# Leaving the last attention step of each tile without a piece of the top-k search, in a one-core hybrid decoder layer

## The chip, the core and the metric

The kernel runs on one core of a Trainium2 chip. The metric is device time in microseconds for one execution of the whole layer; the time of a kernel is the median of several executions, and the profile is a further single execution. TensorE (PE) does the matmuls and the transposes. VectorE (DVE), ScalarE (ACT) and GpSimd (POOL) do the elementwise work, and SyncE (SP) issues the DMAs. Each engine works through its own instructions in the order in which they are written and waits on semaphores for the others.

## What is computed

One decoder layer over 2048 positions of width 1024: a mixing sub-layer (sparse attention beside a pooling mixer), a squared-ReLU MLP, and a gated per-layer embedding. The change touches the sparse attention alone. A cheap indexer scores all keys of a query, the 256 best causal keys are kept, and eight heads attend to those:

```python
logits = jnp.einsum('bqhd,bsd->bqhs', qib, k_idx).astype(jnp.float32) * IDX_SCALE
score = jnp.einsum('bqh,bqhs->bqs', wb.astype(jnp.float32), jax.nn.relu(logits))
causal = key_pos[None, :] <= tq[:, None]
score = jnp.where(causal[None], score, -jnp.inf)
_, sel = lax.top_k(score, n_keep)
...
s = jnp.einsum('bqgrd,bqkgd->bqgrk', qg, kg).astype(jnp.float32) * ATTN_SCALE
s = jnp.where(valid[:, :, None, None, :], s, -jnp.inf)
pr = jax.nn.softmax(s, axis=-1).astype(vg.dtype)
o = jnp.einsum('bqgrk,bqkgd->bqgrd', pr, vg)
```

## The kernel before

The 2048 queries are 16 tiles of 128 (tile 0 to tile 15). The kernel has three stages: the input projection of all tiles, then the attention of all tiles, then the MLP and the embedding in four chunks of 512 rows.

**Attention steps.** Tile i attends to the first 128*(i+1) keys, in blocks of 128 to 512 keys (`blocks`): one block up to tile 3, two in tiles 4 to 7, three in tiles 8 to 11, four from tile 12. One step is one block of one head, so a tile has 8, 16, 24 or 32 steps; `steps` lists all 320, numbered from 0. In step m TensorE makes the scores of a block some two heads ahead (lines 1597 and 1598), transposes the probabilities of step m+2 (line 1682), and multiplies the transposed probabilities of step m with the values (`weigh`, line 1696). VectorE adds the mask to the scores ahead and takes their maximum (`mask_block`, lines 1364 and 1369). ScalarE copies the transposed probabilities of step m from PSUM (line 1012) and takes the exponentials of a later head (line 999).

**What lies beside the steps.** The output projection of the tile before (line 1716) is done by TensorE behind the last block of heads 2 to 5, four matmuls each; these are called output steps below, and the other ones plain steps. At heads 6 and 7 there are transposes of the normalised rows (line 1733), on VectorE at head 7 a scaling (line 1390), and on GpSimd behind that the addition of the residual (line 809).

**The end of a tile.** All heads of a tile gather their outputs in PSUM bank 4. VectorE's `outputs(i)` stands at the start of the first step of tile i+1: it waits for the last `weigh` of tile i, takes the reciprocal of the denominators (line 1375) and writes the scaled outputs to `o_sb` (line 1377). The first `weigh` of tile i+1 writes the same bank, and waits for that (`o_rdy`). The last step of a tile is called its seam below; the one of tile i is `head_first[8*(i+1)] - 1`.

**The search.** Instead of a sort, the limit of the 256 best scores is found bit by bit. For each pair of tiles (t, t+1), t even, there are: two turns of the index queries, the pieces of the index scores ("index", one per head and block: two matmuls, then VectorE's weighing, line 1214, and GpSimd's sum), 32 rounds, a settle and a toggle, and five passes ("pick") for each of the two tiles. In a round VectorE counts the keys of tile t below its limit (line 1227) while ScalarE counts those of tile t+1 (line 910); then VectorE compares both counts (line 1235) and moves both limits (line 1244), which happens in the next step that moves on. The round after it cannot begin sooner. The passes are VectorE's lines 1271, 1276, 1279, 1283 and 1287; GpSimd's line 778 turns the last into a mask, which goes through DRAM. The pairs 2 and 4 are searched beside the input projection; the end of pair 6 and the pairs 8, 10, 12 and 14 are placed in the attention steps 0 to 243.

**What sets the order.** Where a piece goes is worked out when the program is built. Each piece has a cost in units of keys, each step a weight (`step_weight`) of 3.5 units per key of its block plus its share of 1900 for its head. A piece goes to the step where the running sum of weights, scaled to the running sum of costs, reaches its middle; it never goes before the piece ahead of it (`least`), and a first round not before the step after its last index piece. Within a step, each engine does its piece behind its attention work. On VectorE that is: the masks of the blocks ahead, the limits of the round that is pending, the pieces of this step; and in the step after a seam `outputs` comes ahead of all these.

## Time and profile before

| what | value |
| --- | --- |
| median of 3 runs | 3396.7 us (3395.15 to 3403.25) |
| the profiled execution | 3404.94 us |
| its span from the first to the last instruction | 3403.3 us |
| mean granted TensorE clock in it | 0.943 |
| input projection, until the first attention step | about 494 us |
| attention steps with search, tiles 0 to 12 | about 494 to 1366 us |
| attention, tile 13 (the search ends in it) | about 1366 to 1443 us |
| attention without search, tiles 14 and 15 | about 1443 to 1579 us |
| the rest of the span, MLP and embedding above all | about 1579 to 3403 us |

The profile gives the busy time of each engine, the clock that TensorE was granted as a share of its full 2.4 GHz (0.50 is 1.2 GHz), and for each instruction how long its engine sat idle before it, and which instruction ended that. The boundaries between tiles are the starts of the first `weigh` matmul of each.

### The profile page before, as it was taken

To read this page: it belongs to the slowest core of one execution; us is meant where nothing else is said; L and a number is where in the kernel's file an instruction comes from. 1 tells how busy PE (TensorE), PEld (TensorE's weight loads), DVE (VectorE), ACT (ScalarE), POOL (GpSimd) and SP (SyncE) were. 2 spreads that over 40 slices of the span, in tenths; PEclk is the share of its full clock that TensorE was granted. 3 is DMA by queue.
4 is the path that set the end of the run, shared out by engine and by line. 5 is a ranking of instruction groups with operands and counts; after the bars stand their busy time and mean duration, and the time that the engine had idled before them with its cause. 6 is when DMAs were issued, how large, how long until landed. Compare 5 with 4: busy or idle time off the path is not lost.

```text
span 3403.3 us, 38041 instructions
## 1 busy us (share of the span) xinstructions
PE 3059.6 (90%) x13944; PEld 2356.5 (69%) x13944; DVE 1701.9 (50%) x3383; ACT 1332.9 (39%) x2162; POOL 331.2 (10%) x423
## 2 busy tenths in 40 slices
PE   5987877878787887997899999999999999999998
PEld 4876765656665666785688856888668886588873
DVE  3465667777777867731433343333433334333333
ACT  3242427565747556653322222322222222222221
POOL 1322230303030130000000000000000000000000
PEclk9999978888898888999999999999999999999999
DMA  3111122212120110101633312323213323132310
GB/s 121 55 46 48 36 91 59 69 31 70 32 54 27 44 34 19 55 30 57 226 98 99 121 47 75 122 89 99 87 62 119 99 95 98 50 124 87 99 50 25
DMA packets 215456, 250.92 MB, mean 74 GB/s; under 512 B 57952, under 2 KB 160096, under 8 KB 215264
## 3 DMA queue, kind: packets, MB, share of 16 engines
q1 hardware_dynamic: 212960, 239.99, 22.1%
q10 hardware_dynamic: 2304, 8.39, 0.6%
q8 instruction: 118, 1.93, 0.2%
q14 instruction: 74, 0.61, 0.1%
HBM read 208.34 MB, written 40.01 MB: 73 GB/s over the span
## 4 chain that ended last, share of the span: by engine, by line
issue 60%; PE 18%; DVE 7%; ACT 4%; POOL 2%; POOLq 0%; DVEq 0%; ACTq 0%
PE bank L1716 5%; PE bank L1696 5%; PE bank L1597 2%; PE bank L1682 2%; PE bank L1598 2%; PE bank L1575 1%; ACT kept L910 1%; DVE kept L1227 1%; DVE probs L1364 1%; ACT probsT L1012 1%; POOL rstdC L845 1%; DVE too_few L1235 0%; DVE kept L1279 0%; POOL score L821 0%; ACT score_tail L910 0%
## 5 line engine op out<-in xcount | busy, mean ns | idle before, releaser
L1439 DVE TENSOR_TENSOR w_lo<-w_raw,w_hi 128x1024 fp32r<-128x1024 f32 x256 | 312.5, 1221 | 519.8 <-ACT w_hi L1055 514.1
L1055 ACT CAST w_hi<-w_raw 128x1024 fp32r<-128x1024 f32 x256 | 267.3, 1045 | 561.2 <-PE bank L1575 535.1
L1696 PE MATMUL bank<-values,probsT 128*128 128x64 f32 x2176 | 331.4, 299 | 163.5 <-ACT probsT L1012 123.5
L1696 PEld LDWEIGHTS bank<-values,probsT 128*128 128x128 f32 x2176 | 309.6, 217 | 190.3 <-ACT probsT L1012 163.7
L1575 PE MATMUL bank<-hn_hi,w_hi 128*128 128x512 f32 x1024 | 400.0, 391 | 14.1 <-DVE hn_lo L1456 10.7
L1575 PE MATMUL bank<-w_lo,hid_hi 128*128 128x512 f32 x1024 | 405.9, 396 | 0.0
L1575 PE MATMUL bank<-w_hi,hid_lo 128*128 128x512 f32 x1024 | 405.9, 396 | 0.0
L1575 PE MATMUL bank<-w_hi,hid_hi 128*128 128x512 f32 x1024 | 405.9, 396 | 0.0
L1575 PE MATMUL bank<-hn_lo,w_hi 128*128 128x512 f32 x1024 | 399.5, 390 | 0.0
L1575 PE MATMUL bank<-hn_hi,w_lo 128*128 128x512 f32 x1024 | 399.2, 390 | 0.0
L1364 DVE CUSTOM_DVE_ANT_0 probs<-bank,mask 128x384 f32<-128x384 f32 (+3 forms) x320 | 193.7, 607 | 238.0 <-PE bank L1598 237.6
L910 ACT ACTIVATE kept<-score,threshold 128x1024 bf16<-128x1024 f32 (+4 forms) x160 | 252.0, 1575 | 115.1 <-DVE threshold L1244 85.8
L1227 DVE TENSOR_SCALAR_CACHE_REDUCE kept<-score,threshold 128x896 bf16<-128x896 f32 (+4 forms) x160 | 267.7, 1673 | 0.7
L1716 PE MATMUL bank<-wo_sb,mixT_t 128*128 128x512 f32 x512 | 249.4, 633 | 2.3 <-ACT h_t L977 1.5
L1575 PE MATMUL bank<-w_in_hi,hnT_hi 128*128 128x512 f32 (+1 forms) x512 | 196.5, 384 | 46.3 <-DVE hnT_lo L1148 46.3
L1474 DVE CAST hid_hi<-square 128x512 fp32r<-128x512 f32 x128 | 54.6, 426 | 365.5 <-ACT square L1080 365.5
L1078 ACT ACTIVATE square<-bank 128x512 f32<-128x512 f32 x128 | 76.5, 598 | 403.1 <-PE bank L1575 403.1
L1575 PEld LDWEIGHTS bank<-hn_hi,w_hi 128*128 128x128 f32 x1024 | 192.9, 188 | 56.0 <-issue 15.5
L1844 PE MATMUL bank<-w_gate_sb,h3T 128*128 128x512 f32 x512 | 227.4, 603 | 0.0
L1575 PEld LDWEIGHTS bank<-w_hi,hid_lo 128*128 128x128 f32 x1024 | 192.8, 188 | 47.0
L1575 PEld LDWEIGHTS bank<-w_lo,hid_hi 128*128 128x128 f32 x1024 | 192.9, 188 | 47.0
L1575 PEld LDWEIGHTS bank<-w_hi,hid_hi 128*128 128x128 f32 x1024 | 192.9, 188 | 46.9
(191 smaller groups left out, 4776.3 us busy)
## 6 DMA issues: line engine op xcount, KB each, us to landing
w_raw<-in_w_up SPq DMA_DIRECT2D x64, 1024.0 KB, 5.5
w_raw<-in_w_down SPq DMA_DIRECT2D x64, 1024.0 KB, 5.0
x_in<-in_x SPq DMA_DIRECT2D x16, 512.0 KB, 3.7
q_t<-q_scratch SPq DMA_DIRECT2D x32, 256.0 KB, 3.7
x_t<-in_x SPq DMA_DIRECT2D x16, 512.0 KB, 4.4
h_scratch<-h_t SPq DMA_DIRECT2D x16, 512.0 KB, 2.9
hnT_scratch<-hn2T_t SPq DMA_DIRECT2D x16, 512.0 KB, 3.9
hn_lo<-hnT_scratch SPq DMA_DIRECT2D x4, 2048.0 KB, 11.3
```

The lines of the kernel that those rows point to most:

```text
L910: nc.scalar.activation(junk[:, 0:P * (t + 2)], score_of(t + 1), ACT.Sign, scale=-1.0, bias=threshold[:, 1:2].bitcast(F32), accum_out=below ...
L1055: nc.scalar.copy(w_hi[:, p % 4, :].rearrange("p (k f) -> p k f", f=piece_width(p)), raw_piece(p)).then_inc(w_hi_rdy, 1)
L1078: nc.scalar.activation(square[:, f % 2, :], bank[:, UP[q % 2][f % 2], :], ACT.Relu).then_inc(relu2_step, 1)
L1227: nc.vector.tensor_scalar(junk[:, 0:P * (t + 1)], score_of(t), threshold[:, 0:1].bitcast(F32), -float(P), ALU.is_lt, ALU.add, accum_out=be ...
L1364: nc.vector.tensor_tensor_reduce(out=probs[:, H % 3, o:o + w], in0=bank[:, ring_bank[("s", H, b)], 0:w], in1=mask[:, i % 2, o:o + w], scal ...
L1439: nc.vector.tensor_tensor(out_p, raw_piece(p), hi_p.bitcast(F32), ALU.subtract).then_inc(w_lo_rdy, 1)
L1575: ins = nc.tensor.matmul(dst, lhs[a], rhs[b], start=(first and n == 0), stop=(last and n == 2))
L1597: nc.tensor.matmul(dst, hi, k_parts[:, key, o:o + w], start=True, stop=False)
L1598: return nc.tensor.matmul(dst, lo, k_parts[:, key, o:o + w], start=False, stop=True)
L1696: last = nc.tensor.matmul(bank[:, 4, h * HEAD:(h + 1) * HEAD], probsT[:, m % 3, a * P:(a + 1) * P], values[:, kt, HEAD * kv:HEAD * (kv + 1 ...
L1716: last = nc.tensor.matmul(bank[:, mix_bank(i, n), :], mixT_t[:, k, :], wo_sb[:, k, n * 512:(n + 1) * 512], start=(k == 0), stop=(k == K - 1))
L1844: last = nc.tensor.matmul(bank[:, (2, 4)[n], :], h3T[:, a % 2, k, :], w_gate_sb[:, k, n * 512:(n + 1) * 512], start=(k == 0), stop=(k == K ...
```

## The change

The seams of tiles 0 to 14 get the weight 0 in the running sum, so the scale gives their share to all other steps. And a piece that would still fall on a seam goes one step further. So no turn, index piece, round, settle, toggle or pass stands in a seam. The pieces themselves, their order and the code of every engine are as they were. The pending round's limits (lines 1235 and 1244) are still moved in the seam, because that is not a piece with a place of its own.

```diff
@@ -402,7 +402,8 @@
             return 3.5 * blocks[H // Q_HEADS][b][1] + 1900 / len(blocks[H // Q_HEADS])
 
         late = range(0, head_first[Q_HEADS * 13 + 5])
-        weights = np.cumsum([step_weight(m) for m in late])
+        seams = {head_first[Q_HEADS * i] - 1 for i in range(1, T)}
+        weights = np.cumsum([0 if m in seams else step_weight(m) for m in late])
         ends = np.cumsum([cost for _, _, cost in search[n_early:]])
         least = 0
         for (kind, args, cost), e in zip(search[n_early:], ends):
@@ -410,6 +411,8 @@
             if kind == "round" and args[1] == 0:
                 least = max(least, spot_of[("index", args[0] + 1, len(blocks[args[0] + 1]) - 1, IDX_HEADS - 1)] - EARLY_SPOTS + 1)
             least = max(m, least)
+            if least in seams:
+                least += 1
             put(EARLY_SPOTS + least, kind, args)
 
         q_turn_at = {}
```

Thirteen seams lie among the steps with search: steps 7, 15, 23, 31, 47, 63, 79, 95, 119, 143, 167, 191 and 223. Before, they held, in this order: one round, two rounds, three passes (6/4, 7/0 and 7/1, that is tile/number of pass), one round, one round, two passes (9/0 and 9/1), one round, one round, two index pieces, nothing, one pass (12/2), one round and one round. After, all are empty. Among the other steps the pieces move by up to three steps: up to the middle of tile 12 most come later than before. Steps with two rounds in one go from 23 to 24: in output steps from 11 to 8, in plain steps from 11 to 16, and in a seam from 1 to 0. Steps without any piece, seams apart, go from 25 to 18. Output steps that hold index pieces go from 10 to 13. The last piece, pass 15/4, stays in step 243.

In the rows that follow, of the order in which the instructions stand on an engine, the lines of the changed kernel are 3 higher.

VectorE at the end of tile 1 (step 15 and the start of step 16), before:

```order
L1235 TENSOR_SCALAR too_few<-below 128x2
L1244 SCALAR_TENSOR_TENSOR threshold<-too_few,next_tried 128x2
L1390 SCALAR_TENSOR_TENSOR h2_t<-h2_t,rstdB,g_post_row 128x1024
L1225 TENSOR_SCALAR next_tried<-threshold 128x2
L1227 TENSOR_SCALAR kept,below<-score,threshold 128x896
L1235 TENSOR_SCALAR too_few<-below 128x2
L1244 SCALAR_TENSOR_TENSOR threshold<-too_few,next_tried 128x2
L1225 TENSOR_SCALAR next_tried<-threshold 128x2
L1227 TENSOR_SCALAR kept,below<-score,threshold 128x896
L1375 RECIPROCAL inv_denom<-denom 128x8
L1377 TENSOR_TENSOR o_sb<-bank,inv_denom 128x512
```

And in the changed kernel:

```order
L1238 TENSOR_SCALAR too_few<-below 128x2
L1247 SCALAR_TENSOR_TENSOR threshold<-too_few,next_tried 128x2
L1393 SCALAR_TENSOR_TENSOR h2_t<-h2_t,rstdB,g_post_row 128x1024
L1378 RECIPROCAL inv_denom<-denom 128x8
L1380 TENSOR_TENSOR o_sb<-bank,inv_denom 128x512
```

The two rounds between the scaling and the reciprocal are gone from there.

VectorE at the end of tile 5 (steps 62 and 63 and the start of step 64), before:

```order
L1390 SCALAR_TENSOR_TENSOR h2_t<-h2_t,rstdB,g_post_row 128x1024
L1283 SCALAR_TENSOR_TENSOR drop<-kept,drop 128x1152
L1287 SCALAR_TENSOR_TENSOR drop<-score,threshold,drop 128x1152
L1364 ISA probs,block_max<-bank,mask 128x512
L1364 ISA block_max 128x1
L1369 TENSOR_REDUCE neg_max<-block_max 128x1
L1271 TENSOR_SCALAR kept,above<-score,threshold 128x1280
L1276 TENSOR_SCALAR drop<-score,threshold 128x1280
L1375 RECIPROCAL inv_denom<-denom 128x8
L1377 TENSOR_TENSOR o_sb<-bank,inv_denom 128x512
```

And in the changed kernel:

```order
L1393 SCALAR_TENSOR_TENSOR h2_t<-h2_t,rstdB,g_post_row 128x1024
L1274 TENSOR_SCALAR kept,above<-score,threshold 128x1152
L1279 TENSOR_SCALAR drop<-score,threshold 128x1152
L1367 ISA probs,block_max<-bank,mask 128x512
L1367 ISA block_max 128x1
L1372 TENSOR_REDUCE neg_max<-block_max 128x1
L1378 RECIPROCAL inv_denom<-denom 128x8
L1380 TENSOR_TENSOR o_sb<-bank,inv_denom 128x512
```

The passes behind the last masks (9/0 and 9/1) are gone from the seam; the step ahead now holds passes 8/0 and 8/1, where 8/3 and 8/4 stood.

VectorE in the plain steps 81 and 82, in heads 0 and 1 of tile 7, of the changed kernel:

```order
L1238 TENSOR_SCALAR too_few<-below 128x2
L1247 SCALAR_TENSOR_TENSOR threshold<-too_few,next_tried 128x2
L1228 TENSOR_SCALAR next_tried<-threshold 128x2
L1230 TENSOR_SCALAR kept,below<-score,threshold 128x1408
L1398 TENSOR_SCALAR msB<-ssB 128x1
L1367 ISA probs,block_max<-bank,mask 128x512
L1367 ISA block_max 128x1
L1238 TENSOR_SCALAR too_few<-below 128x2
L1247 SCALAR_TENSOR_TENSOR threshold<-too_few,next_tried 128x2
L1228 TENSOR_SCALAR next_tried<-threshold 128x2
L1230 TENSOR_SCALAR kept,below<-score,threshold 128x1408
L1238 TENSOR_SCALAR too_few<-below 128x2
```

The pair of rounds now begins in step 82; before, the pair stood in step 81 and step 82 had one round. In tile 7 such pairs stood in steps 81, 87 and 92, and stand now in steps 82, 86, 89 and 93; of these, 87 and 89 are output steps.

## Rows read from the trace of the kernel before

**Rows 1.** The page: busy tenths of the span in 40 slices, and TensorE's granted clock.

```profile
PE   5987877878787887997899999999999999999998
...
DVE  3465667777777867731433343333433334333333
...
PEclk9999978888898888999999999999999999999999
```

**Rows 2.** Who waited for whom, 494 to 1420 us: total us, times, longest us.

```profile
DVE probs L1364 <- PE bank L1598: 151.6, 76, 7.6
PE bank L1696 <- ACT probsT L1012: 123.3, 82, 3.9
...
PE bank L1696 <- DVE o_sb L1377: 37.7, 10, 10.0
```

**Rows 3.** Timeline, end of tile 1: start us, us, engine, line, operation [idle before, releaser].

```profile
555.06 0.49 PE L1682 MATMUL bank<-ident,probs 128*128 128x128 f32 x3
...
555.65 1.14 DVE L1227 TENSOR_SCALAR_CACHE_REDUCE kept<-score,threshold 128x896 bf16<-128x896 f32 x1
...
558.42 1.14 DVE L1227 TENSOR_SCALAR_CACHE_REDUCE kept<-score,threshold 128x896 bf16<-128x896 f32 x1
...
559.48 0.20 DVE L1375 RECIPROCAL inv_denom<-denom 128x8 f32<-128x8 f32 x1
...
560.55 0.66 PE L1696 MATMUL bank<-values,probsT 128*128 128x64 f32 x2 [5.00 <-DVE o_sb L1377]
```

**Rows 4.** Timeline, end of tile 9, whose seam holds no piece before either.

```profile
1070.91 0.20 DVE L1375 RECIPROCAL inv_denom<-denom 128x8 f32<-128x8 f32 x1 [1.50 <-PE bank L1696]
...
1072.99 0.78 PE L1696 MATMUL bank<-values,probsT 128*128 128x64 f32 x6
```

**Rows 5.** Timeline, end of tile 5.

```profile
763.33 1.35 DVE L1283 SCALAR_TENSOR_TENSOR drop<-kept,drop 128x1152 bf16<-128x1152 f32 x1
763.49 3.39 POOL L809 TENSOR_TENSOR h_t<-h_t,x_t 128x1024 f32<-128x1024 f32 x1 [1.40 <-DVE h_t L1390]
764.71 3.38 DVE L1287 SCALAR_TENSOR_TENSOR drop<-score,threshold,drop 128x1152 bf16<-128x1152 f32 x1
...
768.81 1.54 DVE L1271 TENSOR_SCALAR_CACHE_REDUCE kept<-score,threshold 128x1280 bf16<-128x1280 f32 x1
...
771.07 0.20 DVE L1375 RECIPROCAL inv_denom<-denom 128x8 f32<-128x8 f32 x1
...
772.13 1.08 PE L1696 MATMUL bank<-values,probsT 128*128 128x64 f32 x4 [10.03 <-DVE o_sb L1377]
```

**Rows 6.** Timeline, the ends of tile 2 and of tile 10.

```profile
602.75 0.66 PE L1696 MATMUL bank<-values,probsT 128*128 128x64 f32 x2 [7.30 <-DVE o_sb L1377]
...
1157.61 3.68 DVE L1279 TENSOR_TENSOR_SCAN kept<-drop,above 128x1664 f32<-128x1664 bf16 x1
...
1162.26 1.08 PE L1696 MATMUL bank<-values,probsT 128*128 128x64 f32 x4 [5.66 <-DVE o_sb L1377]
```

**Rows 7.** Timeline of two rounds back to back in step 6.

```profile
517.40 1.14 DVE L1227 TENSOR_SCALAR_CACHE_REDUCE kept<-score,threshold 128x896 bf16<-128x896 f32 x1
...
519.15 1.14 DVE L1227 TENSOR_SCALAR_CACHE_REDUCE kept<-score,threshold 128x896 bf16<-128x896 f32 x1
```

**Rows 8.** Groups by shape, 494 to 1420 us: busy us, mean ns | idle before.

```profile
L1227 DVE TENSOR_SCALAR_CACHE_REDUCE kept<-score,threshold 128x1920 bf16<-128x1920 f32 x32 | 70.6, 2206 | 0.1
...
L1227 DVE TENSOR_SCALAR_CACHE_REDUCE kept<-score,threshold 128x1408 bf16<-128x1408 f32 x32 | 53.5, 1673 | 0.1
```

**Rows 9.** Windows: stretch, us, busy PE, PEld, DVE, ACT, POOL (instructions), PEclk, DMA.

```profile
841.60:846.90 5.30, 2.02 (x15) 1.66 (x15) 4.78 (x15) 4.74 (x7) 0.29 (x1) 1.00 0.22 63
...
866.50:872.30 5.80, 5.50 (x23) 3.21 (x23) 5.59 (x16) 4.95 (x8) 0.00 (x0) 1.00 0.14 28
```

**Rows 10.** Windows behind the ends of tiles 1 and 10.

```profile
560.50:569.20 8.70, 7.22 (x30) 6.66 (x31) 6.71 (x27) 8.05 (x17) 0.55 (x1) 0.50 0.22 76
...
1162.30:1168.80 6.50, 6.50 (x29) 5.92 (x30) 5.87 (x8) 2.15 (x3) 0.84 (x1) 0.54 0.01 4
```

## The prediction

> **What bounds the kernel now.** I read the page first, for where the change can act at all. Pieces of the search stand in steps up to about 1420 us. Behind that TensorE is busy in nine tenths or more of every slice and nothing of it is touched; in the slices of 494 to 1420 us it is busy in seven to nine tenths, VectorE in six to eight, and the granted clock is 0.8 to 0.9 instead of full [rows 1]. So neither engine alone bounds this stage: they hold each other up in turns. The list of waits says how. VectorE waits 151.6 us, 76 times, for scores from TensorE; TensorE waits 123.3 us, 82 times, for ScalarE's copy of transposed probabilities, which stands behind a count of the search; and ten times, 37.7 us in all, TensorE waits at the start of a tile for `o_sb` [rows 2]. The last is what the change aims at. In the timeline of the end of tile 1 the reader sees it: TensorE's last work begins at 555.06 and takes 0.49, VectorE does two more rounds, the reciprocal comes at 559.48, and TensorE goes on at 560.55 after 5.00 us idle [rows 3]. At the end of tile 9, where the seam is empty already, VectorE waits 1.50 us for TensorE and TensorE waits for nothing [rows 4].
>
> **What goes away at the seams.** Seven of the ten waits are small seams with a round or two, or index pieces: 37.7 less the three large ones, 7.30, 10.03 and 5.66, leaves 14.7 us [rows 2, 5, 6]. There VectorE comes to the reciprocal late by about the piece alone. In tile 1 the reciprocal could stand where the first count begins, at 555.65; the 1.07 us from reciprocal to matmul stay (559.48 to 560.55), so TensorE would go on at 556.7 instead of 560.55, and 1.1 us of the 5.00 are left [rows 3]. For the other six I leave 0.6 us together, since tile 9 leaves none [rows 4]. Gain: 14.7 - 1.7 = 13.0 us.
>
> The three large waits have more behind them than the seam's own pieces: VectorE is behind with the passes of the steps ahead, and those steps stay full. In tile 5 the seam loses passes 9/0 and 9/1, 768.81 to 771.07, 2.3 us; the step ahead has 8/0 and 8/1 (like 9/0 and 9/1, 2.2) in place of 8/3 and 8/4 (1.35 + 3.38 = 4.7), a further 2.5 less [rows 5]. The steps before hold a round and a settle in place of three passes, about the same. Left of 10.03: about 5.5 (4.5 to 7). In tile 10 the seam loses the scan of 3.68, but the three steps ahead take on a round and settle later, some 1.6 us more by the counts of about 1.9 at this width: left 3.6 of 5.66 [rows 6, 8]. In tile 2 three passes near 1.3 us go, less half a microsecond for the same reason: left 4.0 of 7.30 [rows 6]. Gain: 23.0 - 13.1 = 9.9 us. Together 22.9 us, with 37.7 as the upper end and 17 as the lower (nothing of the steps ahead gained in tile 5, the small seams half a microsecond each).
>
> **What the moved pieces cost elsewhere.** No piece is dropped, so VectorE and ScalarE do all of it in other steps. First its size on VectorE. Two rounds back to back stand 1.75 us apart with a count of 1.14, so a round is its count plus 0.6 [rows 7]; the counts grow to 1.67 at 1408 keys and 2.21 at 1920 [rows 8]. Seams hold three rounds at 896 keys (3 x 1.75 = 5.2), two at 1152 (2 x 2.0 = 4.0, between the measured widths), two at 1408 (2 x 2.3 = 4.6) and two at 1920 (2 x 2.8 = 5.6): 19.4. The six passes are 3.7 (scan), 2.3, and three near 1.3 each, 9.9 [rows 5, 6]. Two index pieces are put at about 1. Sum: 30 us.
>
> How much of the 30 us shows? A piece dropped into an ordinary step delays VectorE until the next time that VectorE would have waited for TensorE anyway. If TensorE is held up by ScalarE's copy before that, the piece costs its whole length; if VectorE's own wait comes first, nothing. The two kinds are about equally frequent, 82 against 76 [rows 2]. So half, 15 us. The ends are 0 (all of it goes where VectorE idles) and 30 (it meets a held-up TensorE every time). Half also fits the shape of single steps: a pair of rounds in the plain step from 841.6 leaves TensorE busy 2.02 of 5.30 us, the pair in the output step from 866.5 leaves it busy 5.50 of 5.80 [rows 9]. The order says that pairs go from 11 to 16 in plain steps and from 11 to 8 in output steps, which speaks for more than half; empty plain steps are filled (25 to 18 empty), which speaks for less. I stay at half.
>
> The queues that do not carry the sum: GpSimd's sums of index pieces and its last pass of each mask move with the pieces by up to three steps, SyncE's index query loads and mask stores with them; each has its consumer a tile or more later, as the last pass, in step 243, is where it was. If that cover were gone it would show as a wait of line 1364 for a mask load. TensorE's two index pieces (four matmuls) leave the seam of tile 8 and are done elsewhere, at the same length: nothing. Output steps with index pieces rise by three, where TensorE has both and VectorE idles; that is inside the range of the half.
>
> **The clock.** Behind the wait of tile 1 the granted clock is 0.50 (the lower level, 1.2 GHz) for 8.7 us, with TensorE busy 7.22 of them; behind that of tile 10 it is 0.54 for 6.5 us [rows 10]. At the higher level that work would take half. I credit only the one behind a wait that nearly goes away, tile 1: 7.22 / 2 = 3.6 us. The upper end is 10 us (the same for tiles 2, 5 and 10 too), the lower is minus 8, if the five further pairs in plain steps, each with 3.3 us idle [rows 9], lower the clock as the seams did. The Trainium skill ("TensorE: Matmul & The Clock Gate", What's actually happening) holds that the slow clock is the default and activity lifts it; by that rule a seam wait that is merely moved into five more gaps lifts nothing, and the clock credit would be 0, so the time 3.6 us longer.
>
> **Sum.** -22.9 + 15 - 3.6 = -11.5 us against the profiled execution's own span of 3403.3, so 3391.8. The profile stands 8.2 us above the median (3404.94 to 3396.7); I take the difference off the median: 3385.3.
>
> One place speaks of more. In tile 5 the pass of line 1287 takes 3.38 us beside GpSimd's addition of 3.39 us, where line 1283, on the same shape, took 1.35 [rows 5]. The Trainium skill ("SBUF — State Buffer", Who interferes with whom) says that a VectorE instruction with two SBUF inputs is held off by a GpSimd instruction that reads SBUF. The changed order puts 8/0 and 8/1, with one SBUF input each, beside that addition; by the rule some 2 us more would be gained, 3383.3. The trace agrees on the 3.38; that 8/1 is free of it no row shows, so the sum leaves it out.
>
> **The rivals.**
>
> *The moved pieces hide.* If the steps that take them are mostly those in which VectorE idled, only 5 of the 30 us show: -22.9 + 5 - 7 (clock) = -25, 3372 us. For it: the 151.6 us that VectorE waits for TensorE, five times what is moved [rows 2], and the filled empty steps. Against it: the extra pairs stand in plain steps.
>
> *VectorE's chain is the real bound.* Then the waits at the seams were only the place where its lateness showed, and all 30 us come back as waits of line 1696 for line 1012: -22.9 + 30 = +7, less a little clock, some 3402. For it: rounds cannot overlap each other, and in tiles 0, 4 and 7 nearly every step carries a round. Against it: the same 151.6 us.
>
> *Pairs bunch in plain steps.* All 30 us show, and each of the five further pairs also leaves TensorE idle for 3.3 us in one piece [rows 9], behind which the next step or two run at 1.2 GHz, about 1.5 us each: +7 + 8 = +15, 3412 us. It decides as soon as more than about 23 us of the 30 show, with the clock not better. This is the one that ends slower. That the change does not do what it says is ruled out by the order: all thirteen seams are empty.
>
> **Chances.** Forecast 0.45 (3378 to 3394), hiding 0.2, VectorE's chain 0.2, bunching 0.15. A measurement of this kernel can tell about 0.3%, 10 us, from no change: 3386.5 and below is faster, 3406.9 and above slower. Half of the forecast's case lies beyond the first (0.23), with hiding 0.43; the other half and VectorE's chain make 0.41; slower 0.16. The range takes in hiding and most of bunching: 3368 to 3409.
>
> **What the profile after would show.** Right, if line 1696 waits for `o_sb` about 15 us in all (4 to 6 in tile 5, about 1 in tile 1), if its waits for line 1012 grow from 123.3 by some 15 us, if VectorE's waits for line 1598 shrink by some 10, and if everything behind 1443 us has its old length. Wrong on the exposure, if the waits for line 1012 grow by 25 us or more (VectorE's chain, or bunching when the granted clock of 494 to 1366 us is lower too) or by under 7 (hiding). Wrong on the residue, if the wait in tile 5 stays near 10 or goes to nothing.

## The result: slower by 0.7%

| | before | changed |
| --- | --- | --- |
| median | 3397.8 us (3395.15 to 3403.25) | 3421.5 us (3419.9 to 3425.9) |
| ratio | | 1.007, interval 1.0052 to 1.0087 |
| span of the profiled execution | 3403.3 us | 3418.8 us |
| attention steps with search (tiles 0 to 13) | 948.6 us | 965.6 us |
| the span behind them | 1959.9 us | 1960.0 us |

The forecast was 3385.3 us, 3368 to 3409. The time lies above the range. One execution of e10 below took 7896 us, counts as slow and is left out of its ratio. All lines of the changed kernel are 3 higher than in the kernel before.

### The profile after

The page, with the digits that answer to [rows 1]: little can be seen there. TensorE's busy tenths are hardly other than before, and in the slices with search the granted clock is a tenth lower in two (the 12th and 16th) and a tenth higher in two (the 10th and 15th).

```profile
PE   5987878878897888898799999999999999999998
...
DVE  3465667677777777841333343333433333333333
...
PEclk9998978889888897999899999999999999999999
```

The waits between 494 and 1420 us (who waited for whom: total us, times, longest us), which answer to [rows 2]:

```profile
DVE probs L1367 <- PE bank L1601: 158.0, 75, 5.8
PE bank L1699 <- ACT probsT L1015: 134.7, 83, 5.8
...
PE bank L1699 <- DVE o_sb L1380: 17.3, 8, 4.2
PE bank L1600 <- DVE qi_lo L1180: 7.5, 4, 2.5
```

The wait for `o_sb` fell from 37.7 to 17.3 us, as the change meant. The timelines of the ends of tiles 1 and 5 (start us, us, engine, line, operation, [idle before, releaser]) answer to [rows 3] and [rows 5]:

```profile
554.78 0.20 DVE L1378 RECIPROCAL inv_denom<-denom 128x8 f32<-128x8 f32 x1
...
555.85 0.87 PE L1699 MATMUL bank<-values,probsT 128*128 128x64 f32 x3 [0.47 <-DVE o_sb L1380]
```

```profile
764.89 1.41 DVE L1274 TENSOR_SCALAR_CACHE_REDUCE kept<-score,threshold 128x1152 bf16<-128x1152 f32 x1
...
765.05 2.35 POOL L812 TENSOR_TENSOR h_t<-h_t,x_t 128x1024 f32<-128x1024 f32 x1 [1.40 <-DVE h_t L1393]
...
766.22 1.79 DVE L1279 TENSOR_SCALAR drop<-score,threshold 128x1152 bf16<-128x1152 f32 x1
...
769.81 0.85 PE L1699 MATMUL bank<-values,probsT 128*128 128x64 f32 x6 [4.16 <-DVE o_sb L1380]
```

Tile 1: 0.47 us where 5.00 stood. Tile 5: 4.16 where 10.03 stood. Yet the steps became longer. Two places show how.

**At tile 1 the wait moved by one step.** Windows (stretch, us, busy time with the number of instructions of PE, PEld, DVE, ACT and POOL, granted clock, DMA share and GB/s) behind the end of tile 1, which answers to [rows 10]:

```profile
555.80:562.10 6.30, 3.22 (x13) 2.76 (x13) 4.82 (x16) 4.27 (x8) 2.05 (x2) 0.50 0.57 187
555.80:564.50 8.70, 5.62 (x23) 5.16 (x24) 6.27 (x20) 6.67 (x12) 2.05 (x2) 0.50 0.41 136
```

The two rounds of the seam now stand in the first step of tile 2. TensorE is idle for half of its first 6.3 us, and the clock is at 0.50 (1.2 GHz) behind the end of tile 1 as it was before. By steps: 5.00 us of idle time became 0.47 in the seam, 1.43 became 3.03 in the step behind it, and 1.80 became 3.07 in the step ahead, which took on a round too. Tiles 1 and 2 together are 4.1 us shorter, not the 8 that their two seam waits fell by.

**Output step 87** is the one whose window from 866.5 stands in [rows 9]. Before it held a pair of rounds, took 5.80 us and ran at full clock. Now the pair stands in the plain step ahead, and the output step:

```profile
870.50:878.80 8.30, 8.29 (x23) 4.91 (x24) 2.50 (x9) 3.82 (x7) 0.00 (x0) 0.64 0.00 0
```

TensorE is busy all 8.3 us, at a mean clock of 0.64, with VectorE busy for 2.5. There is no idle time in this step to be seen in any list of waits: the loss stands in TensorE's busy time.

### Where the 17 us are

Because busy time hides the clock, I split each trace's attention steps with search (from the first `weigh` of tile 0 to that of tile 14) in three: TensorE's idle time; its *half-clock cost*, which is half of the time that it is busy while the granted clock is at 1.2 GHz; and the rest, which is its work at full clock. Idle times of under 0.15 us are left with the work here, so busy time by the table is 0.6 to 0.8 us more than in the windows. The whole stretch in one window each, before and then after:

```profile
494.80:1443.40 948.60, 776.59 (x3995) 598.14 (x3995) 714.02 (x1736) 588.64 (x986) 164.17 (x147) 0.86 0.16 47
```

```profile
493.20:1458.80 965.60, 795.15 (x3995) 607.82 (x3995) 715.65 (x1736) 590.77 (x986) 162.19 (x147) 0.85 0.16 47
```

| us | length | idle for `o_sb` | idle, all else | half-clock cost | work at full clock |
| --- | --- | --- | --- | --- | --- |
| before | 948.6 | 37.7 | 133.7 | 107.1 | 670.1 |
| changed | 965.6 | 17.3 | 152.4 | 125.3 | 670.6 |
| difference | +17.0 | -20.4 | +18.7 | +18.2 | +0.5 |

TensorE executes the same 3995 matmul records with the same full-clock work and is idle about as long as before, 169.7 against 171.4 us. It is busy 18.6 us longer because 42 stretches at 1.2 GHz hold 250.6 us of its work, where 31 held 214.2. By kind of step: seams -21.5 us, plain steps +14.1, output steps +24.5, of which 12.5 is half-clock cost (24.7 to 37.2), 5.9 idle time and the rest index pieces that came in. Of the output steps with rounds in tiles 4 to 12, six ran below 0.8 of the clock before, thirteen after (two more of before stood at 0.80).

The two profiled executions are 15.4 us apart (3404.94 and 3420.38), as the stretch also begins 1.6 us earlier in the changed kernel. The medians are 23.7 apart, since the profiled execution of before was 7 us above its median and that of the changed kernel was 1.2 below. The traces can't place those 8 us.

### The profile page after: what moved, and what is told of

The parts are those of the page before. It is cut to its first block, busy times and chain, and to the rows that moved or that the text cites. A ratio compares the mean times of both kernels' runs of the same rounds, so it can differ in the third digit from the quotient of the medians.

```text
span 3418.8 us, 38041 instructions
## 1 busy us (share of the span) xinstructions
PE 3076.6 (90%) x13944; PEld 2364.6 (69%) x13944; DVE 1704.0 (50%) x3383; ACT 1335.3 (39%) x2162; POOL 329.6 (10%) x423
## 4 chain that ended last, share of the span: by engine, by line
issue 58%; PE 20%; DVE 7%; ACT 4%; POOL 2%; DVEq 0%; POOLq 0%; ACTq 0%
PE bank L1719 6%; PE bank L1699 5%; PE bank L1600 2%; PE bank L1685 2%; PE bank L1601 2%; PE bank L1578 1%; ACT kept L913 1%; DVE kept L1230 1%; DVE probs L1367 1%; ACT probsT L1015 1%; POOL rstdC L848 1%; DVE too_few L1238 0%; POOL score L824 0%; ACT score_tail L913 0%; DVE threshold L1247 0%
## 5 line engine op out<-in xcount | busy, mean ns | idle before, releaser
L1578 PE MATMUL bank<-hn_hi,w_hi 128*128 128x512 f32 x1024 | 400.0, 391 | 14.1 <-DVE hn_lo L1459 10.8
L1719 PE MATMUL bank<-wo_sb,mixT_t 128*128 128x512 f32 x512 | 260.9, 658 | 3.2 <-ACT h_t L980 2.1
## 6 DMA issues: line engine op xcount, KB each, us to landing
hn_lo<-hnT_scratch SPq DMA_DIRECT2D x4, 2048.0 KB, 11.4
```

Source lines behind the costliest of these rows:

```text
L1578: ins = nc.tensor.matmul(dst, lhs[a], rhs[b], start=(first and n == 0), stop=(last and n == 2))
L1719: last = nc.tensor.matmul(bank[:, mix_bank(i, n), :], mixT_t[:, k, :], wo_sb[:, k, n * 512:(n + 1) * 512], start=(k == 0), stop=(k == K - 1))
```

## Experiments

Each kernel is compared with before on the same chip. The ratio is followed by its interval. "Idle" and "clock" are the split above for the same stretch, from one profiled execution; it lies within 6 us of the kernel's median everywhere but in before (7 us above) and e11 (10 us above).

### Is it the empty seams, the new scale, or any shift?

e1 keeps the weights of before and only moves a piece that falls on a seam one step on. e2 gives the weight of a seam back within its own tile. e3 empties the last step of head 6 instead and leaves the seams full. e4 empties nothing and only changes the share of a head.

e1, against before:

```diff
+        seams = {head_first[Q_HEADS * i] - 1 for i in range(1, T)}
...
+            if least in seams:
+                least += 1
```

e2, against the changed kernel (`lo` and `hi` are the first steps of the tile of m and of the next):

```diff
-        weights = np.cumsum([0 if m in seams else step_weight(m) for m in late])
...
+            whole = sum(step_weight(n) for n in range(lo, hi))
+            return 0 if m in seams else step_weight(m) * whole / (whole - step_weight(hi - 1))
...
+        weights = np.cumsum([open_weight(m) for m in late])
```

e3, which is the change with another set, and e4, against before:

```diff
+        seams = {head_first[Q_HEADS * i - 1] - 1 for i in range(1, T)}
```

```diff
-            return 3.5 * blocks[H // Q_HEADS][b][1] + 1900 / len(blocks[H // Q_HEADS])
+            return 3.5 * blocks[H // Q_HEADS][b][1] + 2300 / len(blocks[H // Q_HEADS])
```

> One part of the change alone: the weights are those of the kernel before, and only the pieces that fall on a seam go one step on, to the first step of the next tile. Every other piece stands where it stood. Theory 'clock' (the seams' waits are gained, but TensorE's idle time comes back in short pieces in plain steps, behind which it works at half clock): the wait for o_sb falls to about 15 to 20 us, TensorE's idle time in the attention stage stays near 171 us, its busy time rises by 5 to 15 us, and the kernel is within 0.3% of before or slightly slower, about 3400 to 3410 us. Rival 'placement' (the kernel before had a lucky alignment of all rounds with the output steps, which the new scale spoils): nothing else is moved, so the seams' gain stays, 3380 to 3390 us.

> The seams are empty as in the change, but each tile keeps its own share of the search: the weight of a seam goes to the other steps of its own tile alone. Rival 'drift' (the change moves pieces over tile boundaries, by which tiles 4, 5, 9 and 10 became longer and tiles 3, 6 and 11 shorter): about as fast as before or faster, 3385 to 3400 us. Theory 'clock' and rival 'placement': like the change, 3410 to 3425 us.

> The same edit at another step: the last step of head 6 of each tile (a plain step) is left without pieces in place of the seam, the seams keep theirs. As many steps are emptied and the scale changes as much. Rival 'placement': as slow as the change plus the seam waits that are not gained, 3420 to 3440 us. Theory 'clock': the pieces come from a plain step and go to plain steps, so the short waits are as many as before and the seam waits stay; 3395 to 3410 us.

> No step is emptied; the share of a head in the weight of its steps is 2300 in place of 1900 units, which moves pieces by a step or so all over the stage and nothing else. It measures what a mere shift of the pieces does. Rival 'placement': 15 to 30 us slower than before, about 3410 to 3430 us. Theory 'clock' says nothing of it beyond that the time goes with TensorE's work done at half clock: within 0.3% of before.

| kernel | median, before beside it | ratio | length | idle `o_sb` / else | clock | seams / plain / output against before |
| --- | --- | --- | --- | --- | --- | --- |
| e1 | 3406.5, 3402.3 | 1.0017 (1.0007 to 1.0028) | 947.6 | 15.1 / 159.2 | 103.6 | -24.1 / +29.4 / -6.1 |
| e2 | 3408.3, 3402.3 | 1.0024 (1.0014 to 1.0034) | 952.3 | 21.9 / 143.8 | 117.4 | -17.8 / +20.3 / +1.3 |
| e3 | 3425.6, 3402.3 | 1.0074 (1.0057 to 1.0091) | 967.4 | 28.5 / 146.7 | 123.6 | -4.1 / +1.5 / +21.5 |
| e4 | 3412.6, 3402.3 | 1.0032 (1.0019 to 1.0044) | 958.9 | 43.4 / 132.0 | 113.9 | +7.5 / +8.3 / -5.4 |

The waits of e1, same view as above:

```profile
PE bank L1699 <- ACT probsT L1015: 144.9, 85, 6.7
PE bank L1699 <- DVE o_sb L1380: 15.1, 7, 7.8
```

What follows: with the seams emptied and nothing else shifted (e1 moves 17 of the 341 pieces) the 22.6 us that `o_sb` gives come back as 21.6 us of waits for line 1015 and 4 of others, and the clock cost is no higher than before. Emptying seams gains nothing; by the ratio it costs 2 to 10 us. And e3, with its seams full, is as slow as the change; 299 of its pieces stand in the very steps in which the change has them. So the larger part of the 24 us doesn't come from the seams at all, but from where the rescaled sum put the other pieces, and it stands in the output steps (+21.5 there, +24.5 in the change).

Most expectations were missed. e1 fell in the band of its theory "clock", but not by its mechanism: TensorE's busy time was to rise by 5 to 15 us and fell by 4. e2 lies between the bands of both rivals. e3 is what "placement" said and not "clock". e4, a mere shift of 317 pieces, the other way than in the change, costs 10 us, at the edge of what "clock" allowed and under the 15 to 30 of "placement": another shift costs less than this one.

### Is the loss TensorE's slow clock?

e5 (the changed kernel) and e6 (before) carry useless matmuls of 64 columns, 336 in all, six in a first block of heads 1 to 6 ahead of `weigh` where that step or the one ahead has a round. They keep TensorE busy in places where it would wait.

```diff
+                if b == 0 and 1 <= h <= 6 and any(at["round"].get(EARLY_SPOTS + n) for n in (m - 1, m)):
+                    for _ in range(FILLER):
+                        nc.tensor.matmul(bank[:, 4, 7 * HEAD:], ident[:], ident[:, 0:HEAD], start=True, stop=True)
```

> The changed kernel with useless TensorE work: in the first step of heads 1 to 6 of each tile, where a round is near (56 steps), six further matmuls of 64 columns stand ahead of the weighing, in the place where TensorE waits for ScalarE's copy; their result is overwritten by head 7. That is about 0.7 us of TensorE work in each step, some 39 us in all. Theory 'clock': they fill waits and keep the granted clock up, so TensorE's own work at half clock falls from 251 us by 50 us or more, and the kernel gets no slower, 3400 to 3420 us. If the clock has nothing to do with it: the filler shows where there is no wait, 3430 to 3445 us.

> The same filler in the kernel before. Theory 'clock': the difference between the two kernels comes from the clock alone, so with the filler in both it shrinks to under 12 us; this one 3390 to 3405 us. If the difference has another cause, it stays near 20 us.

e5: 3416.2 against 3400.5, ratio 1.005 (1.0033 to 1.0066). e6: 3426.3, ratio 1.0072 (1.0055 to 1.0089). The windows of the stretch in e5 and then e6:

```profile
490.50:1448.90 958.40, 841.15 (x4668) 671.61 (x4668) 715.10 (x1736) 590.70 (x986) 162.09 (x147) 0.89 0.16 47
```

```profile
496.60:1467.40 970.80, 845.96 (x4668) 678.85 (x4668) 715.42 (x1736) 589.66 (x986) 164.39 (x147) 0.87 0.16 46
```

The same filler costs the kernel before 26 us and the changed kernel nothing (3416.2 beside 3421.5, their ratios' intervals overlap). It adds 69 us of full-clock work to both and takes 48 (before) and 53 (changed) of their idle time. The half-clock cost goes from 125.3 to 101.9 in the changed kernel and stays in the kernel before, 107.1 to 108.0. So e5 came as expected and e6 did not (3390 to 3405 were expected, 3426 came). The order of the two turned round: the stretch of the changed kernel was 17.0 us longer than that of before, and with the filler it is 12.4 shorter. Of these 29 us the half-clock cost makes 24, the idle time the rest. That the filler takes the cost away in one kernel and not in the other isn't explained, so this supports the split and doesn't prove it. The Trainium skill ("TensorE: Matmul & The Clock Gate", What's actually happening) says that the slow clock is the default and that activity lifts it; the trace of e5 agrees, mean clock 0.89 where the changed kernel has 0.85, and that of e6 hardly shows it, 0.87 where before has 0.86.

### Lighter output steps, and a free step ahead of them

e7 (before) and e8 (changed) give the output steps 2000 units of weight more, which draws pieces into them. e9 (changed) and e10 (before) empty the step two ahead of each output step in tiles 8 to 12. e11 (before) empties the step directly ahead. e12 is e10 with 1500 more for the output steps.

The line of the weight in e7 and e8 (`is_out` is true for the last block of heads 2 to 5), and the edit of e10; e9 has the seams in place of `set()`, e11 has `- 2` for `- 3`, and e12 has both edits with 1500:

```diff
-            return 3.5 * blocks[H // Q_HEADS][b][1] + 1900 / len(blocks[H // Q_HEADS])
+            return 3.5 * blocks[H // Q_HEADS][b][1] + 1900 / len(blocks[H // Q_HEADS]) + (2000 if is_out(H, b) else 0)
```

```diff
+        free = set() | {head_first[Q_HEADS * i + h + 1] - 3 for i in range(8, 13) for h in (2, 3, 4, 5)}
+        weights = np.cumsum([0 if m in free else step_weight(m) for m in late])
...
+            while least in free:
+                least += 1
```

> No step is emptied; instead the weight of each output step gets 2000 units more, so that more rounds go to the steps in which TensorE has the output projection and VectorE idles: pairs in output steps 22 (11 before), in plain steps 5 (11 before). If the price of a piece depends on the step that takes it (near nothing in an output step, its whole length and the clock in a plain one), this is faster than before by 10 to 40 us, 3360 to 3390 us. If VectorE's chain is the bound wherever its pieces stand, within 0.3% of before.

> The change and the heavier output steps together: seams empty, pairs in output steps 17, in plain steps 8. Theory 'price by place': the moved pieces now find output steps, so the seams' 15 to 20 us are kept in part: as fast as the variant with full seams or up to 15 us faster, 3350 to 3390 us. Rival 'conserved idle time' (what is taken from one place of TensorE's idle time comes back at another): no gain over the variant with full seams.

> The change, and in tiles 8 to 12 also the step two ahead of each output step without pieces (20 steps more are emptied, so the others are denser still). Theory 'two rounds ahead of an output step': TensorE waits twice in a row, the granted clock falls, and the long output step runs at half clock (7.5 us in place of 5.4 in the runs so far; 13 such output steps in the change, 6 in the kernel before). With the gap these steps in tiles 8 to 12 run at full clock, 5 to 6 us each: 10 to 20 us faster than the change, 3395 to 3408 us. Rival 'squeeze' (each emptied step makes the rest denser and so slower, wherever it is): slower than the change, 3430 to 3450 us.

> The kernel before with the same 20 steps emptied and the seams as they were. Theory 'two rounds ahead': 5 to 12 us faster than before, about 3390 us. Rival 'squeeze': 20 to 40 us slower.

> As the variant before, but the steps directly ahead of the output steps are emptied in place of those two ahead; the same number and the same density. Theory 'two rounds ahead': the clock is lost in the first of the two waits nearly as often (6.6 us per output step so far with a round two ahead and none directly ahead), so this one is 10 to 20 us slower than its sister, 3400 to 3410 us. Rival 'squeeze': the same as its sister within 5 us.

> Both ideas in the kernel before: output steps weigh 1500 units more and the step two ahead of them in tiles 8 to 12 is empty. Theory: the gains add, 3365 to 3385 us, faster than both kernels. Rival 'squeeze': 3395 us or more.

| kernel | median, before beside it | ratio | length | idle `o_sb` / else | clock |
| --- | --- | --- | --- | --- | --- |
| e7 | 3386.5, 3400.5 | 0.996 (0.9946 to 0.9974) | 930.7 | 30.7 / 113.7 | 116.6 |
| e8 | 3401.5, 3400.5 | 1.0002 (0.9993 to 1.0012) | 948.7 | 19.0 / 131.9 | 126.6 |
| e9 | 3413.3, 3397.7 | 1.0034 (1.002 to 1.0049) | 958.0 | 17.7 / 147.1 | 124.8 |
| e10 | 3398.3, 3397.7 | 0.9994 (0.9978 to 1.001) | 942.9 | 39.8 / 109.4 | 128.7 |
| e11 | 3408.3, 3397.7 | 1.003 (1.0017 to 1.0044) | 967.2 | 39.3 / 135.1 | 126.3 |
| e12 | 3386.2, 3397.7 | 0.9954 (0.9936 to 0.9972) | 930.3 | 36.1 / 112.1 | 112.5 |

The waits of e7:

```profile
DVE probs L1367 <- PE bank L1601: 131.6, 77, 5.5
PE bank L1699 <- ACT probsT L1015: 99.2, 81, 5.3
PE bank L1699 <- DVE o_sb L1380: 30.7, 12, 7.5
```

e7 and e12 beat both kernels, by 14 us (9 to 18) and 16 us (10 to 22) against before, with the seams full. Waits for line 1015 fall by a fifth in e7, where twice as many pairs of rounds (22) stand in output steps, in which TensorE has the output projection to do beside them. On top of the change the same weight gives 20 us (e8 against the changed kernel) and only makes good what the change lost; it is 15 us slower than e7, where no loss and up to 15 us of gain were expected. The gains of e7 and e10 were to add up in e12 (3365 to 3385), but e10 has none and e12 gains what e7 does. e9 shows how little a local repair tells: tiles 8 to 12, where the steps were freed, became 35 us shorter than in the changed kernel (434.8 against 469.9), and the other tiles 28 us longer (tiles 3 to 7 20 of them), as the scale pushed the pieces there. That is why e9 gains 8 us and not the expected 10 to 20; its clock cost is that of the changed kernel. e10 frees the same steps in before and ends where it began, where 5 to 12 us were expected: 24 us less idle time outside `o_sb`, 22 more at half clock. e11 is 10 us slower than e10, as its theory said, but not by the clock: its half-clock cost is 2 us lower, its idle time 25 higher, in an execution 10 us above its median. The theory of two rounds ahead holds for the output steps alone: their half-clock cost is 24.7 us in before, 15.9 in e10 and 26.1 in e11. The plain steps took it over, with 74.2, 103.4 and 90.0.

### The price of a piece by where it stands

In the experiments so far hundreds of pieces moved at once. These three leave every piece where it is in the kernel before, and add one VectorE instruction of 2.28 us in twelve steps: the seam, the first step of head 6, or the output step of head 4 of tiles 1 to 12.

```diff
+                if m in extra_at:
+                    nc.vector.tensor_reduce(extra[:, i:i + 1], values[:].rearrange("p t d -> p (t d)"), AX_X, ALU.max)
```

> The kernel before with one further VectorE instruction of about 2.1 us (a maximum over `values`, 128x2048) at the end of the seam step of each of tiles 1 to 12: 12 in all, about 26 us of VectorE work, and every piece of the search where it was. It measures what one piece costs in a seam. Theory (a piece costs by its place: in a seam its whole length): +22 to +28 us, as longer waits of TensorE for o_sb. Rival (a piece shows to one half wherever it stands): about +13 us.

> The same 12 instructions of about 2.1 us in the first step of head 6 of each of tiles 1 to 12, plain steps. Theory (in a plain step three quarters of a piece or all of it shows, because the next thing TensorE needs stands behind it): +18 to +28 us, so emptying seams into plain steps is a wash. Rival (half shows): about +13 us. Second rival (plain steps hide it): +0 to +5 us.

> The same 12 instructions of about 2.1 us in the output step of head 4 of each of tiles 1 to 12. Theory (TensorE has 16 more matmuls' worth of its own work there, so a piece mostly hides, but what VectorE owes comes out partly in the steps behind): 0 to +10 us. Rival (half shows wherever it stands): about +13 us.

The group of the added instruction in e13 (busy us, mean ns | idle before); it is 27.3 or 27.4 us in the other two as well:

```profile
L1423 DVE TENSOR_REDUCE extra<-values 128x1 f32<-128x2048 f32 x12 | 27.3, 2278 | 0.0
```

| kernel | ratio, before 3398.2 | by the median | length of the stretch | its idle time | its clock cost |
| --- | --- | --- | --- | --- | --- |
| e13, seam | 1.0093 (1.0076 to 1.011) | +32.7 us | +26.6 | +15.3 | +12.6 |
| e14, head 6 | 1.0077 (1.006 to 1.0093) | +27.5 us | +21.5 | +7.8 | +14.6 |
| e15, output step | 1.0045 (1.0028 to 1.0063) | +15.0 us | +10.3 | -2.2 | +13.3 |

The seam's price is direct. At nine of the twelve seams the step is 2.17 to 2.23 us longer, at tile 11's 2.04, at tile 8's 1.08, and at tile 9's nothing: there `o_sb` was not waited for [rows 4]. At tile 1:

```profile
564.31 1.52 PE L1700 MATMUL bank<-values,probsT 128*128 128x64 f32 x6 [7.19 <-DVE o_sb L1379]
```

5.00 us had stood there. And e14 has, at the same place, the same wait:

```profile
551.02 2.28 DVE L1423 TENSOR_REDUCE extra<-values 128x1 f32<-128x2048 f32 x1
...
560.50 1.51 PE L1700 MATMUL bank<-values,probsT 128*128 128x64 f32 x6 [7.19 <-DVE o_sb L1379]
```

The instruction at 551.02 stands in head 6, its own step is no longer than before (3.11 us), and the seam behind it pays all 2.19. The seams of tiles 2, 3 and 5 pay the same. In tiles 4 and 6 to 12 the step that took the instruction is no longer either (0.01 us at most), and the steps between it and the seam are, by 0.6 to 4.7 us. VectorE's debt is handed on to a step where TensorE stands still for it, the seam or one ahead of it. So most of what is taken out of a seam and put into a plain step is paid all the same: 21.5 against 26.6 us in the traces, 27.5 against 32.7 in the medians. Only an output step is cheaper, 10.3 us. In e13 the waits for `o_sb` grew by 21.5 us, near the 22 to 28 that were expected as such waits; the clock cost came on top, and the median lies above that band. The rival "half shows wherever it stands" (13) is ruled out for seam and head 6, whose intervals begin at 26 and 20 us; for the output step, expected at 0 to 10, it is not: 15 us by the median, 10.3 in the trace. The surprise is that the output step costs at all: TensorE's idle time doesn't grow there, its half-clock cost does, by 13 us, and it does so in all three.

### The turns in output steps

In the changed kernel the turns of the index queries of two pairs of tiles had come to stand in output steps 69 and 176. The timeline of step 69 (TensorE alone) shows it idle between the transposes of the turn and the first index piece:

```profile
786.28 1.04 PE L1612 MATMUL bank<-ident,qi_t 128*128 128x128 f32 x8
789.39 0.45 PE L1600 MATMUL bank<-k_parts,qi_hi 128*128 128x384 f32 x1 [2.06 <-DVE qi_lo L1180]
```

e16 moves the turns of both pairs one step on, and with them the two index pieces that stood behind them in the same step (one was meant), eight pieces in all.

```diff
+            if kind in ("turn", "index") and args[1:] in ((), (0, 0, 0)) and is_out(*steps[least]):
+                least += 1
```

> The changed kernel, with the turns of the index queries that its new scale put into output steps (69 and 176) one step further on, and the first index piece behind them with them; nothing else moves. Theory (what matters in the output steps is whether TensorE waits or runs slowly there, and the turns are one of the causes, with 2.1 and 2.5 us of idle TensorE in those two steps): -3 to -6 us against the changed kernel, so about 3416. Rival (such a wait is only moved by one step): no change, 3421.

e16 has 3414.0 us, where about 3416 was expected, ratio 1.0049 (1.0033 to 1.0066), against 1.007 for the changed kernel; the intervals overlap. The trace is clearer: steps 69 and 70 together go from 12.9 to 12.0 us, steps 176 and 177 from 15.5 to 12.4, 4.1 us less where the edit is. The other 6 us that its stretch is shorter (955.2) lie in steps with the same pieces as before, such as output steps 152 and 207, which ran at 0.70 and 0.65 in the changed kernel and run at 1.00 here. Its half-clock cost in all is 125.5, as in the changed kernel (125.3): less in output steps, as much more in plain ones.

### Placement or chance?

That steps with the same pieces should run at another clock asked for a second trace of both kernels, unchanged.

> The kernel before, unchanged, for a second trace of it. If what TensorE does in a step follows from the placement, its 52 output steps take again 316 us (within 4) with 6 of them with rounds at a granted clock under 0.8 (5 to 7), and half-clock work costs 107 us (within 4) in the steps of tiles 0 to 13. If the clock in a step is chance from one execution to the next, these differ by 10 us and more while the whole keeps its length.

> The changed kernel, unchanged, for a second trace of it. Placement: output steps again 340 us (within 4), 13 of them with rounds at a granted clock under 0.8 (12 to 14), half-clock work 125 us (within 4), the wait for o_sb 17 us. Chance: output steps anywhere between 316 and 340 us, and what is missing there stands in plain steps.

e17: 3401.2 us beside 3396.9, ratio 1.0003 (0.9986 to 1.002). e18: 3423.0, ratio 1.0067 (1.0042 to 1.0092). In both, the lengths of tiles 0 to 11 are the same as in the first trace to 0.1 us each, and the waits for `o_sb` are 37.7 and 17.4. In tile 12, from step 194 on in e17 and from step 211 on in e18, the clock falls in other steps, and each stretch is 3.1 to 3.2 us longer (951.8 and 968.7; clock cost 110.3 and 129.1; work at full clock as before). Output steps take 316.9 and 343.5 us. Nine of them with rounds are under 0.8 in e17, where 5 to 7 were expected, and fourteen in e18; but of the three new ones in e17 two had 0.80 in the first trace, so the limit was a poor one. In these two kernels it is placement, not chance: up to tile 11 even the clock falls in the same steps. It need not be so in every kernel. The executions of e10 fall into three groups, two of 3386 us at a mean granted clock of 0.946, five of 3396 to 3399 at 0.939 and two of 3406 at 0.937: there the clock of one program differs from execution to execution, by 20 us of its time, and the trace shows one of them. The reach of a placement is long: in e13, behind 2.2 us more in the seam of tile 4, output step 53 in tile 5 runs at 0.76 instead of 1.00, with every piece of the search in place.

## Why the prediction was wrong, step by step

**What bounds the kernel, and the seams: right in the sum, by luck in its parts.** Predicted: 22.9 us less for `o_sb`, about 15 left. Measured: 20.4 less, 17.3 left. The three large waits left 9.2 us where 13.1 were predicted: tile 2 3.46 (4.0), tile 5 4.16 (5.5, 4.5 to 7), tile 10 1.57 (3.6). The small ones left 8.1 where 1.7 were predicted: tile 1 0.47 (1.1), but tile 3 4.10, and tile 11 2.47, at whose end TensorE had not waited before. The two errors nearly cancel.

In tile 5 the passes 8/0 and 8/1 took 1.41 and 1.79 beside GpSimd's addition, and that addition took 2.35 where it had taken 3.39. I had 8/1 free of it, for its one input. It wasn't. The same instruction on the same shape, with nothing of GpSimd's beside it, in the kernel before:

```profile
757.22 0.82 DVE L1276 TENSOR_SCALAR drop<-score,threshold 128x1152 bf16<-128x1152 f32 x1
```

The Trainium skill ("SBUF — State Buffer", Who interferes with whom) says that a VectorE instruction with two SBUF inputs contends with a GpSimd instruction that reads SBUF, and that a `tensor_scalar` can contend too; the trace agrees, for line 1287 took 3.38 beside the addition (1.42 on the same shape without it, in the changed kernel) and 8/1 took 1.79. So a loss of 1.0 us stood where 2.0 had stood, and the wait, which I had put at 5.5, fell 1.3 us further, not the 2 that I had read out of that section.

The new wait in tile 11 has the same addition in it. The short instruction that makes the next limit takes 0.17 us elsewhere; here it lasts until the addition ends:

```profile
1265.13 2.36 POOL L812 TENSOR_TENSOR h_t<-h_t,x_t 128x1024 f32<-128x1024 f32 x1 [3.12 <-DVE h_t L1393]
...
1265.44 2.07 DVE L1228 TENSOR_SCALAR next_tried<-threshold 128x2 int32<-128x2 int32 x1
...
1271.39 0.85 PE L1699 MATMUL bank<-values,probsT 128*128 128x64 f32 x6 [2.47 <-DVE o_sb L1380]
```

In the kernel before no such instruction met the addition at this place.

**The queues that "do not carry the sum": wrong, by 3 us in the sum of the waits for `o_sb`.** I wrote that GpSimd's sums of index pieces have their consumer a tile later. I had named who waits for them, not who is queued behind them. The end of tile 3 after, whose wait was 1.09 us:

```profile
643.06 4.11 POOL L824 TENSOR_TENSOR score<-score,weighed 128x512 f32<-128x512 f32 x3 [3.19 <-DVE weighed L1217]
647.24 0.46 POOL L828 TENSOR_TENSOR score<-score,causal 128x128 f32<-128x128 f32 x1
647.66 0.55 POOL L803 TENSOR_TENSOR rstdB<-msB,minus_half 128x1 f32<-128x1 f32 x1
...
648.24 1.28 DVE L1393 SCALAR_TENSOR_TENSOR h_t<-h_t,rstdB,g_post_row 128x1024 f32<-128x1024 f32 x1 [2.79 <-POOL rstdB L803]
...
650.51 0.63 PE L1699 MATMUL bank<-values,probsT 128*128 128x64 f32 x4 [4.10 <-DVE o_sb L1380]
```

The sums, moved one step later, hold up line 803 on GpSimd, which holds up the scaling of line 1393 on VectorE, behind which stands the reciprocal: an empty seam, and TensorE waits 4.10 us.

**Half of the moved 30 us shows: near in size, not in its reason.** Predicted +15 on other waits. Measured +18.7, of which 11.4 are the waits for line 1015 (134.7; 15 was the mark, 7 and 25 the limits that I had set). The argument behind it, that a piece costs nothing where VectorE would have waited first, was too kind: with the same pieces moved alone, e1 shows 25.5 of the 30 as idle time, and e14 that a piece in head 6 is paid at the seam or in a step ahead of it. That 18.7 came out near 15 in the change is luck. VectorE's waits for line 1601 should have shrunk by 10 and grew by 6 (158.0): TensorE itself had become later.

**The clock: the step that failed.** The prediction's term was a credit of 3.6 us, with ends of -10 and +8; measured +18.2, 22 of the 28.5 us by which the sum was off in the stretch. Put in place of the -3.6, with the measured waits: -20.4 + 18.7 + 18.2 = +16.5, and +17.0 is what the traces show. I priced the clock only behind the waits that go, and, as a rival, behind five more pairs in plain steps. I didn't ask what the rest of the schedule, which the new scale moves by up to four steps (303 of the 341 pieces; I had written three steps), does to the work that is heaviest at 1.2 GHz, an output step: one with rounds takes 5.2 to 5.5 us on the average at full clock, 7.5 where its granted clock is under 0.8. And the credit at tile 1 didn't come: the window above has 0.50 behind the 0.47 us wait as behind the 5.00, and two rounds with 3.03 us of idle time now stand in the next step. The half-clock cost of tiles 1 and 2 went from 8.5 to 7.8. There the rule of the Trainium skill ("TensorE: Matmul & The Clock Gate", What's actually happening), that the slow clock is the default and activity lifts it, was the better guide: I had worked out a credit of 0 by it, and the trace shows 0.7. For the 18.2 it gives no size.

**The rivals.** "The pieces hide" is out. "VectorE's chain is the bound" (3402) with its +5 us fits e1 and e2, which empty the seams and shift less else (17 and 117 pieces; +6 and +8 by their ratios). "Pairs bunch" had the right mechanism, idle time turned into work at 1.2 GHz, in the wrong steps and at half its size: plain steps have 5.2 us more of it, output steps 12.5.

**From the trace to the median: 9 us.** I took 8.2 us off because the profiled execution of before was that far above its median. The changed kernel's was 1.2 below. Executions of before reach from 3391 to 3409, and I should have carried that as width, not as a shift.

**What stays open.** Why the clock cost of the kernel before is so low isn't settled. Of fourteen other kernels here that move a piece or add one (e1 to e4, e7 to e16), thirteen have 112.5 to 128.7 us of it, one (e1) 103.6, and their mean is 120.1, where before has 107.1 and 110.3. Even 27 us of VectorE work in output steps, which adds no idle time, adds 13 us of it. A reading that fits, not shown: the kernel before sits on a good draw, and most changes give that up whatever they do. What in the placement sets the clock of a step is open too: e3 and the change place the pieces much alike and have 123.6 and 125.3, e4 moves as many pieces the other way and has 113.9. Nor did any kernel show a rule by which to place pieces so that this cost falls; e7 and e12 win on idle time in spite of it.

## What to carry to other kernels

When work is taken off a wait that is seen, ask first whether the next step pays for it: here e13 and e14 price the two places 5 us in 27 apart, while steps in which the other engine has its most work were the cheap place (e15, 10 us in 27; e7, 14 us faster). Split a matmul engine's time into idle, work at full and work at half clock before and after; a list of waits alone showed this change as even. And a change of weights moves every piece behind it: test the intended move alone (e1) before judging it, and charge a change to a placement with the clock, here 13 us in the mean of fourteen kernels.

## What the runs showed of the hardware

- Useless matmuls can cost nothing that is clear of noise: with 69 us of them the changed kernel has 3416.2 us beside 3421.5, with 53 us less idle time and 23 less half-clock cost. The kernel before, with the same ones, loses 26 us (e6).
- Two executions of one program agree to 0.1 us in each of twelve tiles of 27 to 98 us, with the clock falling in the same steps, in both kernels that were traced twice; where they part (from step 194 or 211 on), it is by 3 us. Those of e10 stand in groups up to 20 us apart, with mean clocks of 0.946, 0.939 and 0.937.
- 2.2 us of delay on VectorE can change the granted clock of steps one tile later, in either direction: in e13 output step 43 ran at 1.00 instead of 0.74, step 53 at 0.76 instead of 1.00.
- A VectorE instruction of 128x2 elements took 2.07 us in place of 0.17 beside GpSimd's addition of 2.36 us, and ended with it (changed kernel, 1265.44). In tile 5 of the kernel before, the two-input pass of line 1283 began 0.16 us ahead of the addition and took its ordinary 1.35; the addition then took 3.39 in place of 2.36, and the pass behind it 3.38 in place of 1.42.
